# Second attention of a two-block transformer kernel: where the products of a pair of query blocks, the filler steps and the reciprocals stand in each engine's order

## What is computed

```python
log_f = log_sigmoid(f_raw + fgate_b)
fcum = cumsum(log_f)
for blk in range(8):                      # query blocks of 128 rows, every head
    q0, q1 = blk * 128, (blk + 1) * 128
    s = q[q0:q1] @ k[:q1].T * scale
    s = s + fcum[q0:q1, None] - fcum[None, :q1]
    s = where(kpos <= qpos, s, -inf)
    outs.append(softmax(s) @ v[:q1])
```

## Time and profile before

| | us |
|---|---|
| median of 3 runs | 2603.03 |
| the runs | 2605.16, 2603.03, 2601.33 |
| the profiled execution, its own time | 2604.71 |
| its span, first to last instruction | 2602.9 |
| mean granted clock of TensorE | 0.991 |
| second attention, its eight pairs of heads | 1837 to 2340 |

### The profile page before, as it was taken

How to read it: one execution, slowest core, us unless ns; L and a number is a source line. 1 busy time by engine, 2 the same in 40 slices (tenths; PEclk the granted TensorE clock), 3 DMA queues, 4 the chain that set the end, 5 groups by cost and what they waited for, 6 DMA issues and landing times.

```text
span 2602.9 us, 32821 instructions
## 1 busy us (share of the span) xinstructions
PE 2530.3 (97%) x12946; PEld 2120.4 (81%) x12946; DVE 1580.3 (61%) x2413; ACT 1225.1 (47%) x1858; POOL 1134.3 (44%) x759
## 2 busy tenths in 40 slices
PE   5999999999999999999999999999999999999998
PEld 3788898877888888878788888888888888888886
DVE  7554899487555556665833367665666666654333
ACT  4243888344444443342543435543666666642132
POOL 0222444439787863444487234333322222235233
PEclk8999999999999999999999999999999999999998
DMA  6133001322222226553232322222111111167452
GB/s 272 65 121 130 1 1 66 114 79 92 89 81 78 92 102 242 179 174 122 90 117 102 122 73 90 90 84 71 65 49 49 49 59 60 54 213 273 148 184 97
DMA packets 84457, 275.81 MB, mean 106 GB/s; under 512 B 9392, under 2 KB 9520, under 8 KB 84304
## 3 DMA queue, kind: packets, MB, share of 16 engines
q1 hardware_dynamic: 84304, 273.71, 30.0%
HBM read 219.54 MB, written 54.13 MB: 105 GB/s over the span
## 4 chain that ended last, share of the span: by engine, by line
PE 81%; DVE 9%; ACT 5%; DMA 2%; issue 1%; POOL 1%; SPq 0%; DVEq 0%; ACTq 0%; POOLq 0%
PE ps L614 12%; PE ps L616 12%; PE ps L615 12%; PE ps L991 7%; PE ps L992 7%; PE ps L993 7%; PE ps L857 5%; PE ps L834 4%; PE ps L810 2%; PE ps L811 2%; PE ps L1048 2%; DVE wf L3056 2%; PE ps L1049 2%; PE ps L1050 2%; DVE wf L3081 1%
## 5 line engine op out<-in xcount | busy, mean ns | idle before, releaser
L3383 POOL TENSOR_TENSOR hl<-raw,hl 128x1024 fp32r<-128x1024 f32 x161 | 403.9, 2511 | 933.9 <-ACT hl L1407 933.5
L614 PE MATMUL ps<-ht,hl 128*128 128x512 f32 x1552 | 633.4, 408 | 15.0 <-DVE ht L2456 9.9
L616 PE MATMUL ps<-ht,hl 128*128 128x512 f32 x1552 | 608.3, 392 | 0.0
L615 PE MATMUL ps<-ht,hl 128*128 128x512 f32 x1552 | 607.8, 392 | 0.0
L614 PEld LDWEIGHTS ps<-ht,hl 128*128 128x128 f32 x1552 | 293.5, 189 | 75.4 <-DVE ht L2456 9.9
L616 PEld LDWEIGHTS ps<-ht,hl 128*128 128x128 f32 x1552 | 292.8, 189 | 64.1
L615 PEld LDWEIGHTS ps<-ht,hl 128*128 128x128 f32 x1552 | 294.0, 189 | 53.8 <-issue 1.5
L3459 POOL TENSOR_SCALAR wf<-wf,st 128x1024 f32<-128x1024 f32 (+2 forms) x192 | 168.8, 879 | 318.7 <-DVE st L2589 318.7
L1407 ACT ACTIVATE hl<-raw 128x1024 fp32r<-128x1024 f32 x163 | 171.3, 1053 | 178.9 <-PE ps L1050 66.6
L2396 DVE TENSOR_TENSOR ps<-ps,wf 128x512 f32<-128x512 f32 x116 | 80.8, 697 | 152.3 <-PE ps L993 152.1
L834 PE MATMUL ps<-cst,wf 128*128 128x128 f32 x1088 | 151.4, 274 | 3.8 <-POOL wf L3459 3.8
(11 more groups left out here) (287 smaller groups left out, 5314.8 us busy)
## 6 DMA issues: line engine op xcount, KB each, us to landing
raw<-in_wst SPq DMA_DIRECT2D x243, 512.0 KB, 3.6
wf<-scratch_rows SPq DMA_DIRECT2D x32, 512.0 KB, 5.0
scratch_g<-wf SPq DMA_DIRECT2D x22, 512.0 KB, 2.6
wf<-scratch_g SPq DMA_DIRECT2D x44, 256.0 KB, 4.2
wf<-in_xT SPq DMA_DIRECT2D x16, 512.0 KB, 7.7
htf<-in_wst SPq DMA_DIRECT2D x16, 512.0 KB, 15.4
scratch_ys<-wr SPq DMA_DIRECT2D x16, 512.0 KB, 4.5
ht<-scratch_ys SPq DMA_DIRECT2D x32, 256.0 KB, 5.9
```

What stands on the lines that cost most here:

```text
L614: self.op.matmul(out, wh, xh[:, c], start=(j == 0), stop=False)
L615: self.op.matmul(out, wh, xl[:, c], start=False, stop=False)
L616: t = self.op.matmul(out, wl, xh[:, c], start=False, stop=(j == kt - 1))
L3383: self.op.tensor_tensor(K.hl[:, u * 2048 + 1024:u * 2048 + 2048], K.raw[:, i % 3 * 1024:(i % 3 + 1) * 1024], hi.bitcast(F32), ALU.subtract ...
```

## The change

In PE's list the products of a pair of items move one step on, from the end of an even step to the next odd step, between its scores and its fillers; the transposes are then the last of each step. `fills` gets new numbers, the same for all engines and with the same sum. On DVE the reciprocal and the addition of the products now stand between the next maximum and the low part. On ACT the copy of the products moves from the end of an even step to the head of the next, where nothing stood between. POOL and SP change through `fills` alone.

```diff
 def fills(p, s, own=False):
-    if s < 2:
-        return (0, 3 if p == 7 else 2, 3, 3)[s + 2]
     if p == 7 and s > LAST_FILL:
         return {13: 1, 14: 4, 16: 3}.get(s, 0) if own else 0
     if p == 7:
-        return (2, 1, 2, 1, 2, 2, 2, 1, 2, 1, 2)[s - 2]
-    return 2 if s in (4, 6, 10, 12) else int(s < 14)
+        return (2, 1, 1, 1, 2, 1, 4, 1, 4, 1, 3, 1, 1, 1, 3)[s + 2]
+    return (2, 1, 1, 1, 2, 1, 4, 0, 4, 0, 3, 1, 0, 1, 3, 0)[s + 2] if s < 14 else 0
```

```diff
 # PE, attend2
             for s in range(-2, 18):
                 if s + 2 < 16:
                     sc(s + 2)
+                if s >= 3 and s % 2 == 1:
+                    g = 16 * p + s - 2
+                    hi, lo, _ = pt2(K, (g // 2) % 2)
+                    self.back(2, g, (s - 2) % 8, hi, lo, 6 + (s - 2) // 8, True,
+                              (("vstack2", p),))
                 self.fill(fills(p, s, True))
...
                 if 0 <= s < 16:
                     self.turn(2, 16 * p + s, s % 8, 9 + (16 * p + s) % 3, True)
-                if s >= 2 and s % 2 == 0:
-                    g = 16 * p + s - 1
-                    hi, lo, _ = pt2(K, (g // 2) % 2)
-                    self.back(2, g, (s - 1) % 8, hi, lo, 6 + (s - 1) // 8, True,
-                              (("vstack2", p),))
```

```diff
 # ACT, attend2
                 g = 16 * p + s
+                if s >= 3 and s % 2 == 1:
+                    if s == 3 and p:
+                        self.wait_ge(*K.at("stored_ya", p - 1))
+                    self.back(2, g - 2, (s - 2) // 8, (s - 2) % 8, w(22))
                 self.fill(fills(p, s))
...
                     self.soft(2, g + 2, (s + 2) % 8, 9 + (g + 2) % 3, True)
-                if s >= 2 and s % 2 == 0:
-                    if s == 2 and p:
-                        self.wait_ge(*K.at("stored_ya", p - 1))
-                    self.back(2, g - 1, (s - 1) // 8, (s - 1) % 8, w(22))
```

```diff
 # DVE, attend2 (the maximum of s + 2 stands ahead of this)
+                if 0 <= s + 1 < 16:
+                    self.soft(2, g + 1)
+                if s >= 3 and s % 2 == 1:
+                    self.back(2, g - 2, (s - 2) // 8, (s - 2) % 8, w(22))
                 if 0 <= s < 16:
                     self.turn(2, g, s % 8, pt2(K, (g // 2) % 2), True)
-                if s + 2 < 16:
-                    self.soft(2, g + 2)
-                if s >= 2 and s % 2 == 0:
-                    self.back(2, g - 1, (s - 1) // 8, (s - 1) % 8, w(22))
```

## The result

The changed kernel takes 2638.97 us (median of 4 runs, 2637.2 to 2643.34), the kernel before beside it 2604.1 us: a ratio of 1.0137, 95% interval 1.0125 to 1.015. I had forecast no change. It is 35 us slower. The table reads the two profiled executions; the changed kernel's is the longest of its four, so they differ by more, 38.7 us in span.

What follows compares the result with a forecast made beforehand. PE was taken as the bound, 62.59 of 62.80 us of a pair's stage. Seven pairs' -2.9 us and the last pair's +2.3 gave -0.6, so 2602.4 us for the median; range 2599.0 to 2606.0.

Steps and rivals of the forecast that it cites:

- part 4: On DVE, the reciprocal behind the next maximum: charged nothing, with 0 to 0.3 us per pair kept for the range.
- Rival 2: Steps 0, 1, 11: transposes wait for reciprocals if the maximum starts over 0.15 us late; 2608.4 us, chance 0.07 in full.
- Rival 3: Step 8's wait moves to item 8's bank or another step: 2606.7 us; chance 0.15, shared with a part of Rival 2.
- part 1: On PE, products a step later remove the wait in step 8: -0.61 us in each of seven pairs, -4.3 us.
- Part 2: On PE, step -2's first filler waits for ACT's copy of bank 7: net +0.35 us in each of eight pairs.
- 1 to 3: Pairs 0 to 6: -0.61, +0.35 and -0.15 (fewer filler groups) us per pair; about 62.4 us each, not 62.8.
- 5a: Last pair: the z gate's first filler, now inside step 4's four, waits for ACT's tanh: +0.88 us.
- 5b: Last pair, step 6: item 7's reciprocal now stands behind the maximum, so its transposes start later: +0.61 us.
- 5c: Last pair, step 12: the same delay by the reciprocal behind the maximum, with 768 columns: +0.40 us.
- 5: last pair: Last pair: filler and reciprocal waits, step -2's cost and one more filler group together, +2.3 us.

Runs made afterwards that it cites:

- run 1: The changed kernel with DVE's addition of items 14 and 15 in step 17 put back ahead of the last key-projection steps: 2603.14 us, ratio 0.9996.
- run 2: The changed kernel, DVE's list kept, with SP loading the next pair's row sums ahead of its wait for the late addition: 2603.04 us, ratio 0.9996.
- run 3: The kernel before with only the addition of items 14 and 15 moved behind the key-projection steps in step 17: 2649.4 us, ratio 1.0175.
- run 5: The kernel of run 1 with DVE's reciprocals also back at their old place: 2601.64 us, ratio 0.9989.
- run 8: The kernel of run 5 with no filler in step -2 and the last pair's fillers of before: 2598.13 us, ratio 0.9977.
- run 4: The changed kernel with DVE's reciprocals back behind the low part, the addition still late: 2636.36 us, ratio 1.0126.
- run 6: The kernel of run 1 with the fillers of before: 2600.47 us, ratio 0.9988.
- run 7: The kernel before with the new fillers alone, products and reciprocals where they were: 2602.42 us, ratio 0.9993.

## Why the prediction was wrong

**The step that failed** stands at the end of part 4: "Steps 14 to 17 have no scores and the products follow the transposes directly, as before." It is true of PE, for which it was said, and I let it stand for the other engines. The same part says of ACT that its list is unchanged; for DVE I followed the reciprocal through the steps that I took for its tightest, and the addition through none: its new place went into the sum as nothing, without a reason. The addition was moved past `late` in step 17. Three links hang on it: SP's wait, the two row loads queued behind that wait, and the maximum of the next pair. Runs 1, 2 and 3 show each: restored, the loss goes; with only the loads freed, it goes; alone in the old kernel, it comes. The price of the missed step is 35 us, all of the result, and no rival had it. Rival 2 also had PE waiting for work that DVE does late, but for another instruction, at other steps and at 0.75 us per pair; its condition did not arise, since runs 1 and 5 differ by 0.03 per pair in pairs 0 to 6. Rival 3 is disproved as well: no wait of the products or of item 8's bank is left in run 1.

The other steps can be read in run 1, which is the change without this fault. The half clock behind the stops, 15.4 of the 38.9 us, was not in the sum either; it came with the stops.

| step | predicted | measured |
|---|---|---|
| 1: wait in step 8 | -0.61 per pair, nothing in its place | gone; no late product or transpose in pairs 0 to 6 |
| 2: first filler starts behind the first scores | +0.83 | +0.83 |
| 1 to 3, length of pairs 0 to 6 | 62.4 | 62.46, then 62.37 or 62.38 |
| 4: reciprocal, pairs 0 to 6 | 0 | -0.03 (run 5 against run 1) |
| 2: net cost of the fillers in step -2 | +0.35 | +0.33 (run 5 against run 8, which also has one group fewer) |
| 5a: the z gate's first filler | +0.88 | 0.85 + 0.10 |
| 5b and 5c: reciprocals in the last pair | +0.61, +0.40 | +1.0 together (run 5) |
| 5: last pair | +2.3 | +2.26 |
| sum over the stage | -0.6 | -1.0 |

5b is seen in the last pair of run 1, timelines of DVE, POOL and PE as in the earlier trace rows:

```profile
2296.64 0.69 DVE L3222 SCALAR_TENSOR_TENSOR wf<-wf,ps 128x512 f32<-128x512 f32 x1 [2.28 <-ACT wf L2154]
2297.24 0.28 DVE L2576 CUSTOM_DVE_ANT_0 wf<-ps,wf 128x128 f32<-128x128 f32 x1
...
2297.64 0.15 DVE L2587 RECIPROCAL st<-st 128x1 f32<-128x1 f32 x1
...
2297.89 1.12 POOL L3459 TENSOR_SCALAR wf<-wf,st 128x1024 f32<-128x1024 f32 x1 [4.37 <-DVE st L2587]
...
2299.06 1.09 PE L832 MATMUL ps<-cst,wf 128*128 128x128 f32 x8 [0.61 <-POOL wf L3459]
```

The multiply of the z gate, the maximum, the reciprocal 0.40 later, the weighing 0.25 later, 1.12 long, and then the eight transposes: the chain of part 5b, link by link. Part 2's wait in the same run, timeline of PE, beside the earlier trace rows:

```profile
1899.62 0.33 PE L808 MATMUL ps<-wr 128*128 128x128 f32 x1
...
1900.45 0.50 PE L612 MATMUL ps<-ht,hl 128*128 128x512 f32 x1 [0.27 <-ACT wf L2128]
```

In 5a the extra 0.10 is the filler's first product, 0.33 from start to start where one inside a group takes 0.23:

```profile
2286.68 0.50 PE L612 MATMUL ps<-ht,hl 128*128 128x512 f32 x1 [0.69 <-ACT wf L2166]
2287.01 0.40 PE L613 MATMUL ps<-ht,hl 128*128 128x512 f32 x1
```

**The range.** It was built from the bounds of the steps I had costed, and not even all of these: 2602.4 + 3.2 + 2.4 is 2608.0, where I wrote 2606.0. In rival 3 the "cover of 3.3 against 1.8" is worked out nowhere; part 1 itself has a cover of 1.38 and the scores of item 11 against 0.61. Neither slip decides anything here. The steps came out within 0.5 us over the whole stage; the range failed by a step that was not on the list. One look at the words of the change, "a step later", on all four lists that run through step 17, and at SP's wait for the addition, would have put it there, and the trace of before had the start of its price: the subtractions' 4.98 us in DVE's timeline, the loads issued 0.37 behind the store in SP's.

## What to carry to other kernels

When a change moves an instruction by one step, write out each engine's list across the last steps too, where a loop's tail holds other work than its middle, and name who waits for the moved instruction's semaphore; here 0.43 us of work, moved behind 4.98 us of other work and the wait ahead of it, held SP's queue, and through it the head of each pair from 1 to 7. A load that does not depend on a store belongs ahead of the wait for that store: run 2 made the kernel indifferent to the fault.

## What the runs showed of the hardware

A stop of PE of 2.8 us was followed by three windows of 1 us at a granted clock of 0.50, so the stop cost about half as much again as it lasted. The seven stops of the changed kernel, pairs 1 to 7, last 2.8 to 3.8 us. In pairs 1 to 4 the pair loses 1.6 to 1.9 us beyond its stop, in pairs 5 to 7 2.8 to 3.0. The length of the stop does not tell which: pair 4's is 3.56 and pair 5's 2.97. The clock can also fall when PE is at work again. In pair 4 PE goes on at 2109.78, and the columns of the earlier trace rows give:

```profile
2109.78:2111.20 1.42, 1.42 (x7) 0.98 (x8) 1.32 (x8) 1.10 (x4) 0.38 (x1) 1.00 0.56 228
2112.00:2114.00 2.00, 2.00 (x8) 1.52 (x7) 1.06 (x5) 0.40 (x2) 0.52 (x1) 0.50 0.00 0
```

And one stop left the clock alone: in run 4, pair 5, PE stood still for 3.13 us and went on at 1.00. The pair took 65.92 us, 3.5 more than in run 5.

```profile
2174.60 0.44 PE L808 MATMUL ps<-wr 128*128 128x384 f32 x1 [2.96 <-DVE st L2576]
2174.60:2178.60 4.00, 4.00 (x21) 3.06 (x22) 2.13 (x12) 2.24 (x8) 0.96 (x3) 1.00 0.30 122
```

So the same kind of stop cost from 0.4 to 3.0 us beyond its length, and these runs do not show what decides. Where the loads were not late (runs 1, 2, 5, 6 and 7), PE's stops of 0.1 to 0.9 us left the stage at 1.00.
